# Two hybrid transformer blocks in float32 on one core: attention scores as stacked float32r products

## The reference

```python
q = partial_rope(rmsnorm(heads(q), q_g)); k = partial_rope(rmsnorm(heads(k), k_g))
s_own = jnp.einsum('bhqd,bhkd->bhqk', qj, ko) * scale        # d = 64
```

```python
s = jnp.einsum('bhcqd,bhckd->bhcqk', q[:, :, :, q0:q1], k[:, :, :, :q1]) * scale   # d = 64
p = jax.nn.softmax(jnp.where(allowed, s, -inf)); w = p[:, :, 0] - lam * p[:, :, 1]
```

## Time and profile before

| | |
|---|---|
| time, median of 3 runs | 1234.3 us (1233.23 to 1234.85) |
| span of the profiled execution | 1235.1 us |
| mean granted TensorE clock | 0.977 of full speed |
| TensorE busy | 1183.1 us, 96% |
| VectorE busy | 746.3 us, 60% |
| ScalarE busy | 628.6 us, 51% |
| GpSimd busy | 110.4 us, 9% |

### The profile page before, as it was taken

How to read it: one execution, slowest core, us unless ns; L and a number is a source line. 1 busy time by engine, 2 the same in 40 slices (tenths; PEclk the granted TensorE clock), 3 DMA queues, 4 the chain that set the end, 5 groups by cost and what they waited for, 6 DMA issues and landing times.

```text
span 1235.1 us, 17739 instructions
## 1 busy us (share of the span) xinstructions
PE 1183.1 (96%) x6996; PEld 1017.0 (82%) x6996; DVE 746.3 (60%) x1161; ACT 628.6 (51%) x989; POOL 110.4 (9%) x97
## 2 busy tenths in 40 slices
PE   5899989999999999989999999999999899999997
PEld 4778879989887788769998988888977678889776
DVE  3786757555657867476555565567544655675445
ACT  3534555544544534745454445656545446465462
POOL 0323110000001322100000000003000000030000
PEclk9889899999999979999999999999999999999999
DMA  8435235565565424237655545634432445444321
GB/s 280 123 93 175 86 106 174 181 195 183 185 188 174 134 88 137 85 103 219 189 186 185 192 150 171 186 110 136 133 107 103 136 119 181 127 129 128 108 98 68
DMA packets 88619, 180.72 MB, mean 146 GB/s; under 512 B 8648, under 2 KB 19784, under 8 KB 88536
## 3 DMA queue, kind: packets, MB, share of 16 engines
q1 hardware_dynamic: 87240, 175.32, 45.7%
q10 hardware_dynamic: 1296, 4.26, 0.9%
HBM read 178.51 MB, written 1.05 MB: 145 GB/s over the span
## 4 chain that ended last, share of the span: by engine, by line
PE 81%; DVE 9%; ACT 3%; issue 3%; SPq 1%; DMA 1%; POOL 1%; POOLq 0%; DVEq 0%; ACTq 0%
PE bank L728 22%; PE bank L730 21%; PE bank L729 21%; PE bank L844 4%; PE bank L805 2%; DVE w_lo L1511 2%; PE bank L950 1%; PE bank L856 1%; PE bank L849 1%; DVE vecs L1520 1%; ACT w_hi L1151 1%; PE bank L847 1%; SPq L679 1%; PE bank L864 1%; PE bank L865 1%
## 5 line engine op out<-in xcount | busy, mean ns | idle before, releaser
L1511 DVE TENSOR_TENSOR w_lo<-raw,w_hi 128x1024 fp32r<-128x1024 f32 x296 | 366.1, 1241 | 308.5 <-ACT w_hi L1151 305.0
L1151 ACT ACTIVATE w_hi<-raw 128x1024 fp32r<-128x1024 f32 (+1 forms) x320 | 335.0, 1052 | 248.3 <-PE bank L730 214.5
L728 PE MATMUL bank<-h_hi,w_hi 128*128 128x256 f32 x896 | 262.1, 293 | 1.7 <-DVE w_lo L1511 1.7
L729 PE MATMUL bank<-h_lo,w_hi 128*128 128x256 f32 x896 | 257.3, 287 | 0.0
L730 PE MATMUL bank<-h_hi,w_lo 128*128 128x256 f32 x896 | 257.2, 287 | 0.0
L728 PE MATMUL bank<-w_hi,h_hi 128*128 128x512 f32 (+1 forms) x448 | 184.0, 411 | 12.5 <-ACT prm L1224 6.8
L728 PEld LDWEIGHTS bank<-h_hi,w_hi 128*128 128x128 f32 x896 | 176.0, 196 | 3.5 <-DVE w_lo L1511 2.3
L730 PE MATMUL bank<-w_hi,h_lo 128*128 128x512 f32 (+1 forms) x448 | 177.2, 396 | 0.0
L729 PE MATMUL bank<-w_lo,h_hi 128*128 128x512 f32 (+1 forms) x448 | 176.7, 395 | 0.0
L729 PEld LDWEIGHTS bank<-h_lo,w_hi 128*128 128x128 f32 x896 | 175.6, 196 | 0.5
L730 PEld LDWEIGHTS bank<-h_hi,w_lo 128*128 128x128 f32 x896 | 175.3, 196 | 0.0
(11 more groups left out here) (293 smaller groups left out, 1636.7 us busy)
## 6 DMA issues: line engine op xcount, KB each, us to landing
raw<-in_w_in SPq DMA_DIRECT2D x144, 512.0 KB, 3.9
raw<-in_w_ff SPq DMA_DIRECT2D x128, 512.0 KB, 4.0
raw<-in_w_out SPq DMA_DIRECT2D x40, 512.0 KB, 3.2
raw<-in_cmp_w SPq DMA_DIRECT2D x8, 512.0 KB, 5.1
raw<-in_w_in SPq DMA_DIRECT2D x8, 404.0 KB, 3.5
x_sb<-in_x SPq DMA_DIRECT2D x2, 512.0 KB, 5.7
gain<-in_norm_mix ACTq DMA_DIRECT2D x2, 512.0 KB, 5.8
gain<-in_norm_ffn ACTq DMA_DIRECT2D x2, 512.0 KB, 5.4
```

The lines of the kernel that those rows point to most:

```text
L728: pe.matmul(out_ap, s_hi, m_hi, start=start, stop=False, **kw)
L729: pe.matmul(out_ap, s_hi, m_lo, start=False, stop=False, **kw)
L1151: act.activation(slot(w_hi, u), slot(raw, u), ACT.Copy).then_inc(hi_ready, 1)
L1511: dve.tensor_tensor(slot(w_lo, u), slot(raw, u), slot(w_hi, u).bitcast(F32), ALU.subtract)\
```

## The change

For the scores of block 1 and of the differential heads the query is split into its rounded part and the remainder, which are stacked over 128 partitions: a head's query in float32r on its 64 partitions, the remainder on the other 64. The keys are written twice beside each other in `vec`, so that after the turn both halves of the partitions hold the same key; they are split into a rounded part and a remainder. A head's score is then two float32r products over 128 partitions, stacked query by rounded key and stacked query by key remainder, in place of one float32 product over 64.

For this, keys take twice the slots: in block 1 the rotations cover 12 and 8 slots, in block 2 24 in two calls. Turns become 0, 1, 6 at unit 12 (banks 4, 5, 6) and 2, 3, 5 as before; in block 2 six turns at unit 11, in banks 4, 5, 6, 7, 4, 5. A query turn is read by two ScalarE copies and two VectorE subtractions of 64 partitions, a key turn by one of each; VectorE frees the bank. Turn 4 reads the projected columns directly, without copies, and has two transposes.

```diff
+TURN1_BLOCK = {0: 0, 1: 2, 6: 4, 2: 6, 3: 8, 5: 10}
+TURN2_BLOCK = {0: 0, 1: 2, 2: 4, 3: 6, 4: 8, 5: 10}
@@ timeline, block 1
-                if p == 11:
-                    step("vec_b", l, "copy")
                 if p == 12:
                     single(4, "turn", l, 0)
                     single(5, "turn", l, 1)
+                    single(6, "turn", l, 6)
@@ timeline, block 2
             if p == 11:
-                for u in range(4):
-                    single(4 + u, "turn2", l, u)
+                for u in range(6):
+                    single(4 + u % 4, "turn2", l, u)
@@ heads_of
-                moba = [(pair(vecT, h // 2, h), pair(vecT, 2 + h // 2, h), causal_b, col(520 + HD * h), HD, None) for h in range(4)]
+                moba = [(stack_m[:, h, :], (hi_m[:, h, :], lo_m[:, h, :]), causal_b, col(520 + HD * h), HD, None)
+                        for h in range(4)]
...
@@ head_inputs
                     ("att1", "S", 0): [("turn", l, 0), ("turn", l, 1)],
+                    ("att1", "S", 2): [("turn", l, 6)],
-                    ("diff", "S", 0): [("turn2", l, u) for u in range(4)],
+                    ("diff", "S", 0): [("turn2", l, u) for u in range(3)],
+                    ("diff", "S", 2): [("turn2", l, 3)],
+                    ("diff", "S", 4): [("turn2", l, 4)],
+                    ("diff", "S", 6): [("turn2", l, 5)],
@@ head_stage, S
-                        pe.matmul(ps[:, lo:lo + cols], q[:, i * P:(i + 1) * P], k[:, 0:cols], start=True, stop=False)
+                        for n, kn in enumerate(k):
+                            pe.matmul(ps[:, lo:lo + cols], q[:, i * P:(i + 1) * P], kn[:, 0:cols], start=n == 0, stop=False)
@@ ScalarE
+            def stacked_query(key, dst):
+                ps = src(key)[:, :].rearrange("p (c t) -> p c t", c=2)
+                for r in range(2):
+                    b = slice(HD * r, HD * r + HD)
+                    act.activation(dst[b, :, r, :], ps[b, :, :], ACT.Copy).then_inc(turned_hi, 1)
...
-                            if j < 2:
+                            if j == 1:
+                                free(act.activation(vec[:, i, 8:24, :].rearrange("p (s r) d -> p s r d", r=2),
+                                                    ps[:, :].rearrange("p (s d) -> p s d", d=HD).unsqueeze(2).broadcast_to([P, 8, 2, HD]),
+                                                    ACT.Copy, scale=r), key)
...
-                        if u == 3:
-                            act.dma_start(post_gain, post_norm_2[l].partition_broadcast(P)).then_inc(post_loaded, 16)
+                        if kind == "diff" and s[2:] == ("T", 7):
+                            act.dma_start(post_gain, post_norm_2[l].partition_broadcast(P)).then_inc(post_loaded, 16)
@@ VectorE
+            def stacked_query(key, dst):
+                ps = src(key)[:, :].rearrange("p (c t) -> p c t", c=2)
+                for r in range(2):
+                    b, other = slice(HD * r, HD * r + HD), slice(HD * (1 - r), HD * (1 - r) + HD)
+                    n_turned[0] += 1
+                    dve.wait_ge(turned_hi, n_turned[0])
+                    ins = dve.tensor_tensor(dst[other, :, r, :], ps[b, :, :], dst[b, :, r, :].bitcast(F32), ALU.subtract)
+                    if r:
+                        free(ins, key)
+                    else:
+                        link(ins)
...
+                def scaled_twice(dst, s0, n, g):
+                    o = o_tmp[:, 0:NT * n * HD].rearrange("p (i s d) -> p i s d", i=NT, d=HD)
+                    tt(o, rv[:, :, s0:s0 + n, :], v_r[:, :, s0:s0 + n].unsqueeze(3).broadcast_to([P, NT, n, HD]), ALU.mult)
+                    for i in range(NT):
+                        tt(vec[:, i, dst:dst + 2 * n, :].rearrange("p (s r) d -> p s r d", r=2),
+                           o[:, i].unsqueeze(2).broadcast_to([P, n, 2, HD]),
+                           g_vec[:, l, g, :].unsqueeze(1).unsqueeze(1).broadcast_to([P, n, 2, HD]), ALU.mult)
...
-                            scaled(4, 4, 4, 1)
-                            rope(0, 8)
+                            scaled_twice(4, 4, 4, 1)
+                            rope(0, 12)
...
-                            scaled(12, 18, 1, 4)
-                            scaled(14, 20, 1, 5)
-                            link(dve.tensor_copy(vec[:, :, 13, :], vec[:, :, 12, :]))
-                            link(dve.tensor_copy(vec[:, :, 15, :], vec[:, :, 14, :]))
+                            scaled_twice(16, 18, 1, 4)
+                            scaled_twice(18, 20, 1, 5)
...
+                    elif kind == "turn" and s[2] in (0, 2):
+                        stacked_query(s, query_pairs(1, s[2]))
+                    elif kind == "turn" and s[2] in (1, 3, 6):
+                        turned(s, *key_pair(1, s[2]))
...
-                        rope(0, 16)
+                        rope(0, 8, False)
+                        rope(8, 24)
+                    elif kind == "turn2":
+                        if s[2] < 2:
+                            stacked_query(s, query_pairs(2, s[2]))
+                        else:
+                            turned(s, *key_pair(2, s[2]))
```

More of the change, by code:

```diff
@@ L1580, in rope @@
                 tt(a, t[0], t[1], ALU.subtract)
[L1581 removed]
+                ins = dve.tensor_tensor(b, t[2], t[3], ALU.add)
+                if last:
+                    ins.then_inc(vec_ready, 1)
+                else:
+                    link(ins)
             def row_max(name, h):
```

84 lines of the change are left out of this document (53 added, 31 removed).

## The result

The changed kernel is slower: 1251.65 us (median of 4 runs, 1248.57 to 1252.13) against 1233.76 for the kernel before beside it; the ratio of after to before is 1.0119, 95% interval 1.0088 to 1.0149 (the two medians divided give 1.0145, near its upper end, so the loss is 15 to 18 us). The profiled execution took 1251.27 us with a span of 1249.5. The forecast was 1224 with a range up to 1240: wrong in sign, and outside the range. A second measurement, beside later experiments (12), gave 1.0132 [1.0111, 1.0152], 16 us.

What follows compares the result with a forecast made beforehand. TensorE was taken to bound the kernel, except where VectorE paces block 1's first heads. Per layer -7.2 us in block 1 and +2.0 in block 2, twice, made -10.4 and 1224 us, range 1213 to 1240.

Steps and rivals of the forecast that it cites:

- The score products: Score heads: a head falls from 1.42 to 0.64 us on TensorE, a gain of 0.78.
- The first rival: Score heads: the array drains at every mask, a head costs 1.05 and gains only 0.37; 1237 us, chance 0.17.
- The Trainium skill's rule: Score heads: weight loads overlap matmuls only when row groups differ, which would bring a head near 1.05 us; weighed, not followed.
- Block 1, first turn: Block 1: doubled keys and a longer rotation on VectorE make the first turn come 1.1 us later.
- a gain that is not of TensorE: Block 1, scaling and doubling NSA keys: 4.7 us becomes 1.9, ending before GpSimd starts; -2.8 us.
- Block 1, the subtractions of turns 2 and 3: Block 1: later vectors' subtractions fall into conv work with VectorE idle behind, costing nothing; 2.1 us without that cover.
- Block 1, heads 4 to 11: Block 1: TensorE has no idle time, eight heads gain 6.2 us, counted at 85%; -5.3 us per layer.
- Block 2's turns: Block 2: waits and transposes at the turns cost 6.9 us, clock 1.3, heads gain 6.2; +2.0 per layer.
- The post gain's load: Block 2: the load moves from the last turn to the last diff copy and costs nothing.
- The clock: Block 2's turns: the granted clock falls behind waits, +1.3 us per layer, ends 0 and 2.6.
- The third rival: Block 1 stays paced by VectorE in all heads and gives only 1.9 us per layer; 1234.5 us, chance 0.12.
- the 1.9 us of gain in the first stretch: Block 1, heads 0 to 3: the evacuation before the compression products starts about 85.1 instead of 86.97; net -1.9 us.

Runs made afterwards that it cites:

- 12: The changed kernel measured again with nothing altered, beside later runs: 1252.33 us, ratio 1.0132 to the kernel before.
- version 13: Version 9 with the remainder of unit 17 of block 1 on VectorE instead of GpSimd: 1223.16 us, ratio 0.9875 to the kernel before.
- Version 3: The changed kernel with the first four convolution steps all at unit 16, ahead of turns 2, 3 and 5: 1246.60 us, ratio 1.0095 to the kernel before.
- Version 8: Changed kernel with early convolution (unit 16), block 1's turn 3 in bank 4, differential turns apart, last convolution step at unit 21, silu at 24: 1232.07 us, 0.9961.
- 17: The kernel before with only the remainder of unit 17 of block 1 on VectorE instead of GpSimd: 1233.82 us, ratio 0.9965.
- version 4: The changed kernel with unread identity transposes filling TensorE's waits: 1245.88 us, ratio 1.0082 to the kernel before.
- 5: The changed kernel without VectorE's subtractions in block 1, ScalarE writing both query halves rounded: 1243.25 us, ratio 1.0043 to the kernel before.
- 11: The kernel before with the last convolution step at unit 21 and the silu at unit 24: 1235.08 us, ratio 0.9977.
- 16: The kernel before with last convolution step at unit 21, silu at unit 24 and unit 17's remainder on VectorE: 1225.97 us, ratio 0.9911.
- Versions 9: Version 8 with block 2's rotation in two steps, queries at unit 8 and doubled keys at unit 10: 1225.31 us, ratio 0.9918 to the kernel before.

## Why the prediction was wrong

- **The score products** (0.64 us a head): right, 0.67. The first rival, a drain at each mask, is refuted. The Trainium skill's rule in "TensorE: Matmul & The Clock Gate", Part 3, weighed there, does not hold for these full-height products either: the head did not come near 1.05.
- **Block 1, first turn** (1.1 us later): right, 3.24 against 2.11 us of wait; the table's +2.1 between 144 and 168 is this and the 1.0 of four more transposes (2.82 us against 1.80), within the 0.4 to 0.9 of the forecast but for 0.1.
- **Block 1, "a gain that is not of TensorE"** (-2.8): wrong. The evacuation was to start 1.9 us earlier, at 85.1, and started 1.7 later, at 88.64. I moved VectorE's operations by 0.9 us against a GpSimd remainder that I kept at 84.34. GpSimd begins it behind its own small operations, which wait for VectorE and ScalarE, so it moved as well, to 85.90. And the six operations take 2.7 us unblocked (81.21 to 83.95 in version 13), not 1.9. Even with 1.9 the sum did not bear out "they end before GpSimd starts": 82.13 + 0.9 + 1.9 is 84.9, behind 84.34. "SBUF — State Buffer", "SBUF: two separate sides", in the Trainium skill says that whichever of the two engines starts first holds the shared ports for its whole instruction and the other blocks, also for VectorE operations with two inputs in SBUF. The traces agree: a copy of 0.43 us took 2.29 before, two products of 1.08 took 2.85 after. The prediction had the cause of the stall right and its time wrong.
- **Block 1, the subtractions of turns 2 and 3** ("fall into the conv work, behind which VectorE is idle, and cost nothing"): wrong. The idle time was behind the convolution, the subtractions were put ahead of it, each with a wait for a turn and its copy (2.7 and 3.7 us). I priced their 2.1 us of work and not what is queued behind their waits. Version 3 wins 3 to 5 us by the order alone (6 in the table, 9.6 to 3.5 at 3504, from single profiles).
- **Block 1, heads 4 to 11** (85% of 6.2 us per layer): wrong, the largest term. "TensorE has no idle time" was true of layer 1 and said nothing: at head 9's transposes the exponential was ready only 0.4 us ahead of TensorE. In layer 2 it was not even true; TensorE waited there for 1.2 us. Any gain over the slack turns into a wait, here of 3.6 and 3.9 us. Version 8 shows this place with the change (8 us by moving the silu and the step ahead of it), 17 without it (2.8 us of wait as soon as TensorE comes earlier).
- **Block 2's turns** (+6.9 and 1.3 of clock, less 6.2, makes +2.0): right in sum, 1.9 and 2.3, and in its waits, 1.6, 3.0 and 0.4 or 0.8 against 1.8, 3.2 and 1.0. The post gain's load cost nothing.
- **The clock**: counted for block 2 only. Of the 35 us more at the lower level after (92 against 57, by the mean clocks), the forecast had none in block 1; version 4 prices the whole at about 5 us.

The third rival, block 1 paced by VectorE in all its heads, had the mechanism, but it kept the 1.9 us of gain in the first stretch and no price for the order: 1234.5. What stays open: how the 10 us of block 1 divide between the late list, the order and the clock. They are not additive (3 and 4 took 3 to 5 and 4 to 6 us, 5 took 8 to 11 with runs spread over 13 us), and 11, 17 and 16 show that one place hides the next. The wait of 1.6 us for the exponential of head 1 was not looked into by any run.

## What to carry to other kernels

An engine without idle time may still have nothing to gain: go through its dependences in the stretch, take for each the time between the operand's readiness and its use, and cap the gain at the smallest; here 0.4 us in one layer and none in the other, against a forecast of 5.3 in each. An operation that waits for another engine is priced with everything queued behind it on its own engine; put it behind independent work or not at all. When a stall comes from two engines meeting, find out what starts each of them before promising that it goes.

## What the runs showed of the hardware that was not expected

GpSimd pays for a meeting too: beside a convolution step of after that took 3.55 instead of 1.53 us, two of its remainders took 5.16 us, where the same two took 4.73 before.

```profile
117.55 3.55 DVE L1855 SCALAR_TENSOR_TENSOR xn<-arena,prm,xn 128x256 f32<-128x256 f32 x3
...
118.19 5.16 POOL L1464 TENSOR_TENSOR w_lo<-raw,w_hi 128x1024 fp32r<-128x1024 f32 x2 [6.42 <-ACT w_hi L1190]
```

The clock is not the same from one execution to the next: after and version 3 are the same program up to the compression, and the same wait of 1.9 us for its bank was followed by 16 products in 3.60 us in one (above) and in 1.96 in the other:

```profile
87.16 1.96 PE L989 MATMUL bank<-blocksT,raw 128*128 128x15 f32 x16 [1.91 <-DVE arena L1847]
```

The spread of a version's runs goes with this clock. Version 5 took 1234.4 us at a mean granted clock of 0.974 and 1247.8 at 0.966, version 11 1226.4 at 0.985 and 1238.1 at 0.975. Versions 9 and 16, whose four runs lie within 2.2 us, were measured fewer times. Why one version spreads and another does not is open.
